# Upward products of the FFN and of two MLPs: two 256-column products become one of 512 columns, and ScalarE and VectorE add the halves

## The reference, cut to what matters

```python
def swiglu(h, w1, w3, w2):                       # layer 0 of the first block, D_FF = 2816
    return (jax.nn.silu(h @ w1) * (h @ w3)) @ w2

# second block, both layers l, D_FF_2 = 4096
h = rmsnorm(x, norm_mlp_g[l]) * (1.0 + sc2) + sh2
x = x + g2 * (jnp.square(jax.nn.relu(h @ w_up[l])) @ w_down[l])

# the modulation of layer l, whose weights are read ahead of it (see "ada" below)
mod = silu(c) @ w_ada[l] + b_ada[l]              # 1024 x 6144
```

## Time and profile before

| what | value |
|---|---|
| median of 3 runs | 1919.8 us (1919.7 to 1920.91) |
| profiled execution, first to last instruction | 1919.5 us |
| what lies around the span | no more than the 0.3 us between it and the median; the page gives no other time for this execution |
| mean granted TensorE clock | 0.991 of full speed |
| matmuls | 10592 |
| FFN, up and down | about 132 to 322 us of the span |
| first MLP (with ada slots) | about 1394 to 1576 us |
| second MLP | about 1730 to 1912 us |

### The profile page before, as it was taken

How to read it: one execution, slowest core, us unless ns; L and a number is a source line. 1 busy time by engine, 2 the same in 40 slices (tenths; PEclk the granted TensorE clock), 3 DMA queues, 4 the chain that set the end, 5 groups by cost and what they waited for, 6 DMA issues and landing times.

```text
span 1919.5 us, 27067 instructions
## 1 busy us (share of the span) xinstructions
PE 1855.8 (97%) x10592; PEld 1606.9 (84%) x10592; DVE 1527.7 (80%) x2097; ACT 1200.0 (63%) x1650; POOL 46.1 (2%) x56
## 2 busy tenths in 40 slices
PE   8999999999999999999999999899999999999998
PEld 7889998788888888888888887688789988878997
DVE  5768887568999999999999999667589985756565
ACT  4544444646888888888888887567454446744443
POOL 0010000002000000000000010000000000000000
PEclk9999999999999999999999999999999999999999
DMA  8348896755999999999999999343278974315451
GB/s 317 132 165 307 329 346 245 279 203 218 420 389 377 383 377 390 369 391 375 396 368 388 367 403 380 145 154 129 69 272 332 356 278 154 129 70 187 181 192 44
DMA packets 76060, 528.37 MB, mean 275 GB/s; under 512 B 8690, under 2 KB 9074, under 8 KB 14610
## 3 DMA queue, kind: packets, MB, share of 16 engines
q1 hardware_dynamic: 69696, 504.40, 68.4%
q10 hardware_dynamic: 3060, 11.02, 1.6%
q0 software_dynamic: 3168, 11.14, 1.4%
HBM read 515.90 MB, written 11.01 MB: 275 GB/s over the span
## 4 chain that ended last, share of the span: by engine, by line
PE 88%; DVE 5%; ACT 3%; issue 2%; POOL 0%; DMA 0%; POOLq 0%; DVEq 0%; SPq 0%; ACTq 0%
PE ps L563 27%; PE ps L565 27%; PE ps L564 27%; PE ps L793 2%; PE ps L745 1%; DVE w_lo L1416 1%; PE ps L1015 1%; PE ps L758 1%; ACT w_hi L2321 1%; DVE arena L1402 1%; PE ps L580 0%; ACT score L2447 0%; POOL stat L2854 0%; ACT xT L2331 0%; PE ps L998 0%
## 5 line engine op out<-in xcount | busy, mean ns | idle before, releaser
L2321 ACT ACTIVATE w_hi<-ring 128x1024 fp32r<-128x1024 f32 x862 | 911.3, 1061 | 561.7 <-PE ps L565 551.9
L1416 DVE TENSOR_TENSOR w_lo<-ring,w_hi 128x1024 fp32r<-128x1024 f32 x862 | 1040.7, 1222 | 237.2 <-ACT w_hi L2321 224.2
L563 PE MATMUL ps<-w_hi,x_hi 128*128 128x512 f32 (+1 forms) x1056 | 409.5, 390 | 3.7 <-DVE x_lo L2011 1.4
L565 PE MATMUL ps<-w_hi,x_lo 128*128 128x512 f32 (+1 forms) x1056 | 399.7, 381 | 0.0
L564 PE MATMUL ps<-w_lo,x_hi 128*128 128x512 f32 (+1 forms) x1056 | 398.4, 380 | 0.0
L563 PE MATMUL ps<-x_hi,w_hi 128*128 128x256 f32 x1248 | 358.1, 287 | 8.4 <-DVE x_lo L1523 6.1
L564 PE MATMUL ps<-x_lo,w_hi 128*128 128x256 f32 x1248 | 353.7, 283 | 0.0
L565 PE MATMUL ps<-x_hi,w_lo 128*128 128x256 f32 x1248 | 353.6, 283 | 0.0
L563 PE MATMUL ps<-w_hi,h_hi 128*128 128x512 f32 x732 | 285.5, 390 | 2.7 <-DVE h_lo L1428 1.8
L564 PE MATMUL ps<-w_lo,h_hi 128*128 128x512 f32 x732 | 284.9, 389 | 0.0
L565 PE MATMUL ps<-w_hi,h_lo 128*128 128x512 f32 x732 | 284.3, 388 | 0.0
(11 more groups left out here) (297 smaller groups left out, 1283.6 us busy)
## 6 DMA issues: line engine op xcount, KB each, us to landing
ring<-in_stream SPq DMA_DIRECT2D x478, 1024.0 KB, 6.9
x_store<-arena ACTq DMA_DIRECT2D x1, 4096.0 KB, 31.6
arena<-x_store POOLq DMA_DIRECT2D x7, 512.0 KB, 8.3
y_store<-y_slots POOLq DMA_DIRECT2D x7, 512.0 KB, 8.7
con<-in_consts ACTq DMA_DIRECT2D x1, 2048.0 KB, 17.8
arena<-in_ln_rows ACTq DMA_DIRECT2D x3, 512.0 KB, 5.4
resid<-in_x SPq DMA_DIRECT2D x2, 512.0 KB, 5.1
ring<-in_stream SPq DMA_DIRECT2D x2, 512.0 KB, 8.0
```

The source lines that it names most:

```text
L563: pe.matmul(out_, lhs[0], rhs[0], start=start, stop=False)
L565: return pe.matmul(out_, lhs[1], rhs[0], start=False, stop=stop)
L1416: dve.tensor_tensor(lo, ring[:, q % RING, a:a + HALF], hi.bitcast(F32), ALU.subtract)\
L2321: act.activation(half_buffer(m)[0], ring[:, q % RING, a:a + HALF], ACT.Copy).then_inc(hi_ready, 1)
```

## The change

`x_hi` and `x_lo` become two views of one tile `x_both` of 128 x 2 x 8 x 256. A new function `wide_tile` replaces `feature_tile` in the three stages: per part of the contraction one matmul moves the 512 columns x_hi, x_lo over the weights' high part, and one moves the 256 columns x_hi over their low part. A half now fills a whole bank: columns 0 to 255 hold (high + low weights) by x_hi, columns 256 to 511 hold high weights by x_lo. In the FFN the four halves of a step take banks 0 to 3, so up waits per pair of banks until VectorE has read them (`sums_made`). ScalarE copies the second halves of two banks to `xT` (`keep_part`), VectorE adds them to the first halves (`both_parts`), and Silu then works from SBUF; Relu and the square become one VectorE instruction; ScalarE makes `h_hi`. The points at which both engines convert weight halves within a step are set anew.

```diff
+            def wide_tile(m, b):
+                hi, lo = half_slot(m, KT)
+                for k in range(KT):
+                    x_tile(k)
+                    pe.matmul(ps[:, b, :].rearrange("p (v s) -> p v s", v=2), hi[:, k, :], x_both[:, :, k, :],
+                              start=k == 0, stop=False)
+                    last = pe.matmul(ps[:, b, 0:S], lo[:, k, :], x_hi[:, k, :], start=False, stop=k == KT - 1)
                 last.then_inc(half_done, 1)
...
-            def up(n, banks, j, ready):
+            def gated_up(n, j):
+                for s in range(2):
+                    if j >= 1:
+                        pe.wait_ge(sums_made, 2 * (j - 1) + s + 1)
+                    for i in range(2):
+                        wide_tile(2 * (n + s) + i, 2 * s + i)
+
+            def up(n, j, ready):
                 if j >= 2:
                     pe.wait_ge(hid_ready, ready(j - 2))
-                for s, b in enumerate(banks):
-                    for i in range(2):
-                        feature_tile(2 * (n + s) + i, b, i)
+                for i in range(2):
+                    wide_tile(2 * n + i, 2 * (j % 2) + i)
...
-            def hidden(j, ready, done, paired):
-                split_to(2 * done + PAIRS)
-                dve.wait_ge(act_ready, ready(j))
+            def both_parts(out_, b):
+                parts[0] += 1
+                dve.wait_ge(part_kept, parts[0])
+                return dve.tensor_tensor(out_.rearrange("p (a s) -> p a s", a=2), ps[:, b:b + 2, 0:S],
+                                         xT[:, b:b + 2, :], ALU.add)
+
+            def hidden(j, done, paired):
                 p = j % 2
-                other = acth[:, p, :]
-                if paired:
-                    slots_done(done)
-                    other = ps[:, 2 * p + 1, :]
                 if hids[0]:
                     dve.wait_ge(hid_ready, hids[0])
-                link(dve.tensor_tensor(ff[:, 2, :], acth[:, p, :], other, ALU.mult))
-                split(h_hi[:, p, :], h_lo[:, p, :], ff[:, 2, :]).then_inc(hid_ready, 1)
+                if paired:
+                    split_to(reach(2 * (done - 1)))
+                    both_parts(acth[:, p, :], 0).then_inc(sums_made, 1)
+                    split_to(2 * done + 1)
+                    both_parts(ff[:, 2, :], 2).then_inc(sums_made, 1)
+                    dve.wait_ge(sums_made, 2 * j + 2)
+                    dve.wait_ge(act_ready, j + 1)
+                    dve.tensor_tensor(acth[:, p, :], acth[:, p, :], ff[:, 2, :], ALU.mult).then_inc(hid_made, 1)
+                else:
+                    split_to(2 * done + 1)
+                    link(both_parts(ff[:, 2, :], 2 * p))
+                    dve.scalar_tensor_tensor(out=acth[:, p, :], in0=ff[:, 2, :], scalar=0.0, in1=ff[:, 2, :],
+                                             op0=ALU.max, op1=ALU.mult).then_inc(hid_made, 1)
+                split_to(reach(2 * done))
                 hids[0] += 1
+                dve.wait_ge(hid_hi, hids[0])
+                dve.tensor_tensor(h_lo[:, p, :], acth[:, p, :], h_hi[:, p, :].bitcast(F32), ALU.subtract)\
+                    .then_inc(hid_ready, 1)
...
-            def activations(j, done, func, paired):
-                slots_done(done)
-                act.activation(acth[:, j % 2, :], ps[:, (2 if paired else 1) * (j % 2), :], func)\
-                    .then_inc(act_ready, 1)
+            def hidden_hi(j, done, paired):
+                def keep_part(b, end):
+                    split_to(2 * end + 1)
+                    act.wait_ge(half_done, 2 * end)
+                    act.activation(xT[:, b:b + 2, :], ps[:, b:b + 2, S:2 * S], ACT.Copy).then_inc(part_kept, 1)
+                    split_to(reach(2 * end))
+
+                if paired:
+                    keep_part(0, done - 1)
+                    act.wait_ge(sums_made, 2 * j + 1)
+                    act.activation(acth[:, j % 2, :], acth[:, j % 2, :], ACT.Silu).then_inc(act_ready, 1)
+                keep_part(2 if paired else 2 * (j % 2), done)
+                hids[0] += 1
+                act.wait_ge(hid_made, hids[0])
+                act.activation(h_hi[:, j % 2, :], acth[:, j % 2, :], ACT.Copy).then_inc(hid_hi, 1)
```

More of the change, by code:

```diff
@@ L239, in build @@
         w_lo = sb("w_lo", [P, PAIRS, HALF], F32R)
-        x_hi = sb("x_hi", [P, KT, S], F32R)
-        x_lo = sb("x_lo", [P, KT, S], F32R)
+        x_both = sb("x_both", [P, 2, KT, S], F32R)
+        x_hi, x_lo = x_both[:, 0], x_both[:, 1]
         h_hi = sb("h_hi", [P, 2, BANK], F32R)
@@ L415, in build @@
         act_ready = sem("act_ready")
+        part_kept = sem("part_kept")
+        sums_made = sem("sums_made")
+        hid_made = sem("hid_made")
+        hid_hi = sem("hid_hi")
         hid_ready = sem("hid_ready")
@@ L621, in feature_tile @@
                 last.then_inc(half_done, 1)
+            def wide_tile(m, b):
[5 more added lines that the diff above has]
+                    last = pe.matmul(ps[:, b, 0:S], lo[:, k, :], x_hi[:, k, :], start=False, stop=k == KT - 1)
+                last.then_inc(half_done, 1)
             def tiles(n0, count, job0, fresh, first=0):
@@ L826, in swiglu @@
                     if j < J1:
-                        up(n, [2 * (j % 2), 2 * (j % 2) + 1], j, ready)
+                        gated_up(n, j)
                         n += 2
@@ L1362, in _ @@
                     if j < J2:
-                        up(n, [j % 2], j, ready)
+                        up(n, j, ready)
                         n += 1
@@ L1649, in _ @@
             hids = [0]
-            def hidden(j, ready, done, paired):
-                split_to(2 * done + PAIRS)
-                dve.wait_ge(act_ready, ready(j))
+            parts = [0]
+            def both_parts(out_, b):
[4 more added lines that the diff above has]
+            def hidden(j, done, paired):
                 p = j % 2
-                other = acth[:, p, :]
-                if paired:
-                    slots_done(done)
-                    other = ps[:, 2 * p + 1, :]
                 if hids[0]:
                     dve.wait_ge(hid_ready, hids[0])
-                link(dve.tensor_tensor(ff[:, 2, :], acth[:, p, :], other, ALU.mult))
-                split(h_hi[:, p, :], h_lo[:, p, :], ff[:, 2, :]).then_inc(hid_ready, 1)
+                if paired:
[12 more added lines that the diff above has]
+                split_to(reach(2 * done))
                 hids[0] += 1
+                dve.wait_ge(hid_hi, hids[0])
+                dve.tensor_tensor(h_lo[:, p, :], acth[:, p, :], h_hi[:, p, :].bitcast(F32), ALU.subtract)\
+                    .then_inc(hid_ready, 1)
             def keep_heads(gain):
@@ L1868, in _ @@
             for j in range(J1):
-                hidden(j, lambda j: j + 1, W_FFN0 + swiglu_up(j) + 1, True)
+                hidden(j, W_FFN0 + swiglu_up(j) + 1, True)
             def split_ple(layer):
@@ L2288, in _ @@
                 norm(7 + 2 * l, modg[:, 1, :], ada[:, 16:24], next_half=2 * (n0 + B_MLP))
-                base = J1 + l * J2
                 for j in range(J2):
-                    hidden(j, lambda j: base + j + 1, n0 + B_MLP + mlp_up(j) + 1, False)
+                    hidden(j, n0 + B_MLP + mlp_up(j) + 1, False)
                 if l == 1:
@@ L2491, in two_heads @@
                                ps[:, b, :].rearrange("p (t f s) -> p t f s", t=2, f=2), ACT.Copy).then_inc(catT_hi, 1)
-            def activations(j, done, func, paired):
-                slots_done(done)
-                act.activation(acth[:, j % 2, :], ps[:, (2 if paired else 1) * (j % 2), :], func)\
-                    .then_inc(act_ready, 1)
+            hids = [0]
+            def hidden_hi(j, done, paired):
[12 more added lines that the diff above has]
+                act.activation(h_hi[:, j % 2, :], acth[:, j % 2, :], ACT.Copy).then_inc(hid_hi, 1)
             act.wait_ge(resid1_in, 16)
@@ L2543, in _ @@
             for j in range(J1):
-                activations(j, W_FFN0 + swiglu_up(j) + 1, ACT.Silu, True)
+                hidden_hi(j, W_FFN0 + swiglu_up(j) + 1, True)
                 if j == 0:
@@ L2837, in _ @@
                 for j in range(J2):
-                    activations(j, n0 + B_MLP + mlp_up(j) + 1, ACT.Relu, False)
+                    hidden_hi(j, n0 + B_MLP + mlp_up(j) + 1, False)
                     if (l, j) == (0, 0):
```

## The result

The changed kernel takes 1985.5 us (median of 5 runs, 1983.9 to 1987.0) against 1920.9 for the kernel before: 1.0334 times as long, 95% interval 1.0323 to 1.0345. The profiled execution spans 1983.3 us, 63.8 more than the one before.

A forecast was written before the change was run, and what follows sets the result against it. TensorE was taken as the bound (busy 97%, 88% of the chain). Waits of 72.6 us less a gain of 11.2 add 61 us to 1919.5: 1981 us, own range 1954 to 1998, stated range 1938 to 1999.

The forecast's parts named there:

- Order of conversion as the cause: All three stages: weight halves converted only behind the new waits come late and cost TensorE 72.6 us of waits.
- neither engine is a bound by its sum: VectorE and ScalarE: added work, 10.3 us in the FFN and 4 us in the first MLP, bounds neither engine.
- Half E+1 late by 0.89 us in the MLPs: Both MLPs: half E+1 is converted behind the wait, so TensorE waits 0.89 us in 16 steps each, 14.2 us per MLP.
- Half E+2 behind an ada slot: First MLP: an ada slot ahead of half E+2 makes it another 0.72 us late in 13 steps.
- the four terms: FFN step: halves E-1, E, E+1 and E+2 late by 0.50, 0.66, 1.64 and 0.72 us, together 3.52 us.
- Silu and the second copy behind the late addition: FFN: in-order ScalarE waits for the first addition, then does Silu and the second low half; half E+1 is 1.64 us late.
- TensorE's gain of 11.2 us: Up products: 0.347 us per part instead of 0.360, 0.104 us less in each of 108 halves, 11.2 us in all.
- Waits at the stage ends: Last step of FFN and first MLP: `h_lo` behind an ada slot, 2.69 us late against 1.0 now, 1.7 more each.
- the rival of the falling clock: TensorE's clock falls behind waits, some 50 us more if for a quarter of the FFN: 2033 us; chance 6%.
- some 70: Sign in the profile after: TensorE waits on VectorE's `w_lo` of some 70 us in place of 0.6.
- rest absorbed: Rival: only half E+1 is late, 43 x 0.89 = 38.3 us, later terms vanish: 1947 us; chance 10%.
- Faster: Rival: half E+1 ready in time, deciding at 0.21 us lateness per MLP step; 1908 us with no lateness; chance 8%.

The follow-up runs named there:

- the last version: The changed kernel with half E+1 converted ahead of the wait, the FFN's first addition earlier and ada slots folded earlier: 1914.8 us, 0.9963 of the kernel before.
- wide products alone: The kernel before with only the wide products, their high-weights by x-low part left out of the result: 1920.9 us, 0.9998 of the kernel before.
- half E+1 early: The changed kernel with both engines converting one weight half more ahead of each wait: 1930.5 us, 1.0052 of the kernel before.
- the addition first: As half E+1 early, and VectorE makes the FFN's first addition before the ada slot and half E: 1928.3 us, 1.0033 of the kernel before.

## Why the prediction was right

The forecast was 1981 us, measured 1985.5. By its own steps:

- **Order of conversion as the cause: shown.** The new order with the old products loses more than the change does, and converting one half earlier gives nearly all of it back with the new products and additions in place. My reading that neither engine is a bound by its sum held too: the fastest version has the same work on VectorE.
- **Half E+1 late by 0.89 us in the MLPs: right, 0.78 in the step above.** The chain starts a little earlier (the copy at T+0.20, not 0.26). It recurs in every step of both MLPs. The second MLP, which has nothing else, grew by 11.5 us against 10.9; with the 2.3 us that the width gives back there (256 pairs at 0.009) that is 13.8 in 16 steps, 0.86 each. The 0.15 us from VectorE's end to full pace is a slight misreading: the earlier trace rows give 0.06 + 0.11 = 0.17.
- **Half E+2 behind an ada slot, 0.72 us in 13 steps: right, 0.75.** Moving the ada slot alone took 12.5 us from the first MLP (13 x 0.75 = 9.8, the rest from the last wait).
- **FFN, 3.52 us in a full step: the four terms are there, a little smaller.** The starts show 0.28, 0.59, 1.43 and 0.67 above the steady pace, 2.97 together. The slower first step behind each wait, about 0.1, is not in these but is in the forecast's terms: from T0 to the start of half E+2 the step takes 207.39 - 193.04 = 14.35 us, where 16 pairs at 0.351 and 24 long matmuls at 0.227 take 11.07. That is 3.3 us against 3.52. Silu and the second copy behind the late addition were read rightly: T+1.03 against T+1.04 in my chain.
- **TensorE's gain of 11.2 us: too large.** Only some halves have the pace of 0.347 us a pair; most have 0.351 to 0.354. Where wide and short alternate, the wide one starts its successor after 0.234 on average and not 0.227. That makes 864 x 0.006 to 0.009 = 5 to 8 us. With the width undone the three stages were 6.6 us longer; with nearly all waits gone they are 7.6 shorter than before, of which some 1.3 are waits on `h_lo` (1.8 us before, 0.5 in the last version). The prediction says that the trace before has no 512-column matmul followed by one of 256. It has: each up part behind a down part, as at 263.98 and 264.21, 37 undisturbed cases in the three stages, all close to 0.227 apart. Reading them would have confirmed the 0.347, not warned against it. By the rule of the Trainium skill, "TensorE: Matmul & The Clock Gate", section "Back-to-back issue gap", the gain was an estimated 2.2 us; that section gives the formula for isolated matmuls. The measured value lies between it and mine.
- **Waits at the stage ends: right in place (2.47 and 2.46 us idle), short in price.** I took 1.0 us for the wait of now and 2.7 for the new one, so 1.7 more, and left out that the clock could fall there. In the FFN 7 steps of 0.43 instead of 0.23 us follow, in the first MLP 5; with the slower first step each stage end costs some 3 us more than before, of which the clock has about 1.5. So the rival of the falling clock came true, but only in these two places of the changed kernel.

The three stages grew by 64.7 us, and 61.4 were forecast. With a gain of 5 to 8 us instead of 11.2 and some 3 us for the clock, the waits come to 67 to 70 us instead of 72.6: smaller waits and the smaller gain nearly cancel, and the clock makes up the rest. That the total came within 5 us of the forecast is in part this luck. The list of waits shows 42.8 us on `w_lo` and not the "some 70" of the prediction, since it counts from modelled ends. The rival "rest absorbed" failed: every term shows in the starts of a step. "Faster" had its kind of condition right, though at the measured pace it decides at 0.14 us of lateness a step and not at 0.21; the last version, with no such wait inside the stages, meets it. One sum was off without consequence: the forecast's own bounds add up to 2001 at the top (1981 + 3 + 6 + 11), not 1998.

What stays open is why most pairs take 0.351 to 0.354 us and some 0.347. The alternation of widths can't be the whole reason, nor that the wide matmul reads its 512 columns as two separate pieces of `x_both`: both hold in the fast halves too. In the last version, which has nearly no waits, only 3 of 105 halves have the fast pace.

## What to carry to other kernels

When a new wait enters a queue that also prepares another engine's input, list what that queue could already do while it waits, and put it ahead of the wait: here one half more in three `split_to` calls was worth 55 us, the whole idea in its best version 7. Averages of busy time (VectorE 83, 90 and 62% in the three stages before) don't show such a loss; the step chain, instruction by instruction from T on, gave each wait inside the stages to within about 0.2 us. And price a wider matmul from the starts of matmuls in a row, since durations overlap: the removed instruction was worth 0.006 to 0.013 us, not its listed 0.28.

## What the runs showed of the hardware that was not expected

- Where wide and short matmuls alternate (L632 and L634), the wide one is followed after 0.234 to 0.236 us on average (0.230 in the fastest halves, up to 0.241 in others), against 0.227 in the down parts, and the short one after 0.117 instead of 0.120. A short successor alone doesn't do this: in the kernel before, a down part's last matmul is followed by a 256-column one after 0.227.
- Behind TensorE's waits of 2.47 and 2.46 us (changed kernel), 3.12 (wide products alone) and 3.43 (half E+1 early) the clock went to 1.2 GHz for a few matmuls; behind waits of 2.16 to 2.18 us at three stage ends (half E+1 early, and the addition first) it stayed at 2.4 GHz. The length of the wait alone does not decide: behind the same wait of 2.21 us, 53 us into the span, the clock fell in four of the ten profiles and not in the other six, and in the kernel with the old products it fell within 1.4 us behind a wait of 1.97. What does decide is not shown.
- Reading two separate 256-element pieces of PSUM took nearly the same time as one of 512: ScalarE 0.60 us against 0.58, VectorE 0.69 against 0.68.
